# Split query and key products in the scores of a hybrid block, and half of a gate chunk computed earlier

## The reference, cut to what matters

```python
def mla_branch(c_q, c_kv, k_rope, cos, sin, ...):
    q = (rms_norm(c_q, q_norm) @ w_uq).reshape(B, S, 8, 64 + 32)
    q_nope, q_rope = q[..., :64], apply_rope(q[..., 64:], cos, sin)
    kv = (rms_norm(c_kv, kv_norm) @ w_ukv).reshape(B, S, 8, 64 + 64)
    k_nope, v = kv[..., :64], kv[..., 64:]
    k_rope = apply_rope(k_rope, cos, sin)
    s = (einsum('bhqd,bhkd->bhqk', q_nope, k_nope)
         + einsum('bhqr,bkr->bhqk', q_rope, k_rope)) * 96 ** -0.5
    p = softmax(where(key <= query, s, neg))
    return einsum('bhqk,bhkd->bhqd', p, v) ... @ w_o
merged = sigmoid(gate_a) * y_a + sigmoid(gate_b) * y_b
```

## Time and profile before

| | us |
|---|---|
| median of 3 runs | 1553.4 (1551.65 to 1553.79) |
| the profiled execution, its own time | 1557.54 |
| its span in the trace | 1555.8 |
| TensorE busy | 1513.7, 97% |
| VectorE busy | 1080.2, 69% |
| ScalarE busy | 659.0, 42% |
| GpSimd busy | 96.8, 6% |

### The profile page before, as it was taken

The page is one execution under the profiler, slowest core; times in us unless marked ns, Lnnn a source line. Parts: engine busy times, 40 slices in busy tenths (PEclk is TensorE's granted clock), DMA queues, the critical chain, the costliest instruction groups (busy, mean ns, idle before and its releaser), DMA issues.

```text
span 1555.8 us, 26174 instructions
## 1 busy us (share of the span) xinstructions
PE 1513.7 (97%) x10293; PEld 1219.9 (78%) x10293; DVE 1080.2 (69%) x1776; ACT 659.0 (42%) x1165; POOL 96.8 (6%) x181
## 2 busy tenths in 40 slices
PE   6999999999999999999999999999999999999998
PEld 5976666777777888788787887888888888888776
DVE  6468976467786581477866469777777757777786
ACT  7544454344433212445423236444444533333453
POOL 1010000000010001255100020000000000000000
PEclk9999999999999998999999999999999999999999
DMA  5020000713222535302346214444444688888754
GB/s 194 25 67 28 1 1 7 198 41 106 65 68 65 166 122 124 109 4 68 108 162 256 83 48 135 150 149 152 157 154 145 218 307 316 292 289 282 265 186 149
DMA packets 176752, 212.41 MB, mean 137 GB/s; under 512 B 28645, under 2 KB 110946, under 8 KB 176002
## 3 DMA queue, kind: packets, MB, share of 16 engines
q1 hardware_dynamic: 176574, 210.91, 40.9%
q10 hardware_dynamic: 68, 0.02, 0.0%
HBM read 154.11 MB, written 54.82 MB: 134 GB/s over the span
## 4 chain that ended last, share of the span: by engine, by line
PE 72%; DVE 13%; DMA 9%; issue 2%; ACT 2%; SPq 1%; DVEq 0%; ACTq 0%
PE bank L3255 19%; PE bank L2855 17%; DMA down_raw<-in_w_ff_down 6%; PE bank L3319 5%; PE bank L3167 5%; PE bank L3220 5%; PE bank L2755 3%; PE bank L2715 2%; PE bank L2648 2%; PE bank L2768 2%; PE bank L2783 2%; PE bank L2793 2%; DMA z_raw<-in_w_ff_down 2%; DVE yl L2482 1%; DVE mg_lo L2480 1%
## 5 line engine op out<-in xcount | busy, mean ns | idle before, releaser
L2855 PE MATMUL bank<-uT_hi,w_hi 128*128 128x512 f32 x432 | 172.3, 399 | 0.0
L2855 PE MATMUL bank<-uT_hi,w_lo 128*128 128x512 f32 x432 | 169.0, 391 | 0.0
L2855 PE MATMUL bank<-uT_lo,w_hi 128*128 128x512 f32 x432 | 168.9, 391 | 0.0
L3319 PE MATMUL bank<-mg_lo,mg_hi 128*128 128x512 f32 x576 | 135.7, 391 | 2.4 <-DVE mg_lo L2482 2.1
L3319 PEld LDWEIGHTS bank<-mg_lo,mg_hi 128*128 128x128 f32 x576 | 107.5, 188 | 27.8 <-DVE mg_lo L2482 5.6
L3319 PE MATMUL bank<-yh,mg_lo 128*128 128x512 f32 x384 | 119.1, 391 | 0.2
L1259 ACT ACTIVATE zbuf<-bank 128x512 f32<-128x512 f32 x54 | 32.3, 599 | 183.8 <-PE bank L2855 179.7
L2855 PEld LDWEIGHTS bank<-uT_hi,w_hi 128*128 128x128 f32 x432 | 81.6, 189 | 22.1 <-issue 5.2
L1606 ACT ACTIVATE f<-f 128x512 f32<-128x512 f32 x64 | 40.5, 632 | 131.6 <-DVE f L2434 69.6
L2855 PEld LDWEIGHTS bank<-uT_hi,w_lo 128*128 128x128 f32 x432 | 81.7, 189 | 17.4 <-issue 1.0
L2855 PEld LDWEIGHTS bank<-uT_lo,w_hi 128*128 128x128 f32 x432 | 81.6, 189 | 17.4
(11 more groups left out here) (497 smaller groups left out, 3778.4 us busy)
## 6 DMA issues: line engine op xcount, KB each, us to landing
down_raw<-in_w_ff_down SPq DMA_DIRECT2D x80, 512.0 KB, 5.5
down_raw<-f_spill SPq DMA_DIRECT2D x56, 512.0 KB, 4.2
f_spill<-x SPq DMA_DIRECT2D x80, 256.0 KB, 2.6
w_raw<-in_w_in SPq DMA_DIRECT2D x28, 512.0 KB, 4.2
sgate<-gate_spill SPq DMA_DIRECT2D x16, 512.0 KB, 4.4
up_a<-in_w_ff_up SPq DMA_DIRECT2D x16, 512.0 KB, 4.8
up_b<-in_w_ff_up SPq DMA_DIRECT2D x16, 512.0 KB, 4.2
f_spill<-f SPq DMA_DIRECT2D x32, 256.0 KB, 2.3
```

Source lines behind the costliest of these rows:

```text
L2855: ins = nc.tensor.matmul(ps[2 * slot + g][:], st[:, slot, k, :], mv[:, k, g * HALF:(g + 1) * HALF], start=(k == 0 and m == 0), stop=(k == ...
L3319: ins = nc.tensor.matmul(ps[4 * (q % 2) + t][:], st, mv_, start=(start and w == 0 and m == 0), stop=(stop and w == 1 and m == 2))
```

## The change

**Scores.** Each score product becomes three fp32r products with 128 rows. The stationary operands are `qh` (both 64-row halves hold the high part of the query), `ql` (its low part twice) and `qr3` (the rope rows four times, two groups of 32 rows with the high part and two with the low part); the moving ones are `kn` (high part of the key in one half of the rows, low part in the other) and `kr3` (rope rows of the key likewise). The query chunks are copied in one piece with the softmax scale in it, so that DVE's scaling of the maximum (L1904) goes. They are stored to DRAM chunk by chunk (`store_q`), loaded per query tile (`load_q`, two DMAs, and `load_q_rope`, four), and split by GpSimd (`q_split`, four operations for each tile, the tile's chunk of 1024 numbers a partition). The 17 spreading DMAs go. A tile's load waits for the scores of the tile two before. ACT copies a key chunk in two pieces, DVE then subtracts in two.

**Gate chunk.** Half of chunk two (24 matmuls, tokens 0 to 511) moves from behind the last unit into units 22 to 29, three each; its rounding and subtraction move from units 24 and 26 to unit 21. ACT copies the result at unit 31.

**Inverse.** `tt` and `xg` are zeroed whole by GpSimd, SP's loads of `tt` wait for that, and the products take 64 rows instead of 32, the added ones zero.

```diff
-        [(kind, g, j) for j in range(2) for kind in ("x", "rot")] + [(kind, g, j) for kind in ("q", "k") for j in range(NH // 2)]]
+        [(kind, g, j) for j in range(2) for kind in ("x", "rot")] + [(kind, g, j) for j in range(NH // 2) for kind in ("q", "k")]]
-BANKS = (2, 6, 7, 4, 5, 3, 0, 1)
+BANKS = 3 * (2, 6, 7, 4, 5, 3, 0, 1) + (2, 6, 7, 0, 4, 1, 5, 3)
...
+FILL2 = range(22, 30)
...
+                def q_split(i):
+                    b, low = i % 2, slice(2 * ROPE, 4 * ROPE)
+                    pool.wait_ge(*s_qt[b](32 * (i // 2 + 1)))
+                    pch(pool, nc.gpsimd.tensor_scalar(qh[b][:], qn[b][:], 1.0, 0.0, ALU.mult, ALU.add))
+                    nc.gpsimd.tensor_tensor(ql[b][:], qn[b][:], qh[b][:].bitcast(F32), ALU.subtract).then_inc(s_ql.sem, 1)
+                    pool.wait_ge(*s_qrt(64 * (i + 1)))
+                    pch(pool, nc.gpsimd.tensor_scalar(qr3[b][:], qr_in[:], 1.0, 0.0, ALU.mult, ALU.add))
+                    pool.wait_ge(*s_ql(i + 1))
+                    nc.gpsimd.tensor_tensor(qr3[b][low], qr_in[low], qr3[b][low].bitcast(F32), ALU.subtract).then_inc(s_rl.sem, 1)
...
-                for m in range(2):
-                    nc.gpsimd.memset(tt[CH * m + BL:CH * m + CH, :, 0:BL], 0.0).then_inc(s_z0z, 1)
+                nc.gpsimd.memset(tt[:], 0.0).then_inc(s_z0z, 1)
+                nc.gpsimd.memset(xg[:], 0.0).then_inc(s_z0z, 1)
...
-                        ins = nc.tensor.matmul(ps[b0 + g][:, 0:w], qT[0:QH, h, i * P:(i + 1) * P],
-                                               kT[0:QH, h, 512 * g:512 * g + w], start=True, stop=True)
+                    if h == 0:
+                        pe.wait_ge(*s_ql(i + 1))
+                        pe.wait_ge(*s_rl(i + 1))
+                    terms = ((qh[b][:, at[0], at[1], :], kn[:, h, :]), (ql[b][:, at[0], at[1], :], kn[:, h, :]), (qr3[b][:, h, :], kr3[:]))
+                    for m, (st, mv) in enumerate(terms):
+                        for g in range(halves(u)):
...
+                    if u in FILL2:
+                        if u == FILL2.start:
+                            pe.wait_ge(s_wcl, KD + 3)
+                        j = 3 * (u - FILL2.start)
+                        fill(3, 0, j, j + 3)
...
-                fill(2, 0, 0, 6)
+                fill(3, 1, 0, 6)
                 values(n)
...
-                fill(2, 0, 6, 3 * KD)
-                fill(3, 1, 0, 3 * KD)
+                fill(3, 1, 6, 3 * KD)
...
-                            rows = slice(CH * m + BL, CH * m + CH)
+                            rows = slice(CH * m, CH * m + CH)
```

171 lines of the change are left out of this document (122 added, 49 removed).

## The result

| | before | after |
|---|---|---|
| median of 22 runs each, in turn on one chip, us | 1553.12 (1548.49 to 1557.63) | 1558.18 (1550.76 to 1559.98) |
| ratio, 95% interval | | 1.0027 (1.0019 to 1.0035) |
| the profiled execution, its own time / its span | 1557.54 / 1555.8 | 1557.32 / 1555.6 |
| first mask of attention / mask of unit 63 | 112.37 / 261.66 | 115.52 / 270.77 |
| first product of the windows | 279.43 | 285.48 |

The change makes the kernel slower by 0.27%. I forecast 1547.6, a gain of 0.4%, in a range that ends at 1552.5. The forecast was wrong, and the time lies outside the range.

A forecast was written before the change was run, and what follows sets the result against it. TensorE, busy 97% of the span, was taken as the bound, with DVE's chain counting in T2 to T4. The terms summed to -5.8 us, giving 1547.6 from the median of 1553.4; range of 8 in 10: 1539.5 to 1552.5.

The forecast's parts named there:

- T5 to T7, -7.0: Attention tiles T5 to T7: cheaper score products save 0.24 to 0.34 us a unit, all of it TensorE's; minus 7.0 us.
- T4, -1.2: Attention tile T4, bound by DVE: without L1904 the chain is 0.15 us shorter a unit; minus 1.2 us.
- The way of the queries: Stores, loads and GpSimd's splits of queries: 11.2 us a tile, covered by a tile of attention; costed at nothing.
- The first split under the last projections: Before attention: GpSimd's first query split lies under the 24 last projections; costed at nothing.
- Unit 21, +3.0: Weight rounding moved to unit 21: weights land late and ACT, DVE, TensorE wait; plus 3.0 us (1.2 to 4).
- T3, +0.8 and +0.4 for units 22 and 23: Gate matmuls inside units: units 22 and 23 plus 0.4 us; T3, with units 24 to 29 at 2.32 us, plus 0.8.
- Behind attention, -2.8: After the last unit: 24 matmuls fewer are 5.5 us, but TensorE waits for the weight load; 2.8 us saved.
- +0.9 for the clock: Ahead of the first window: the 2.7 us pause can lower TensorE's clock; half of 1.7 us taken, plus 0.9.
- T0 and T1, units 16 to 20: Early attention: T0 plus 0.5 us (0 to 1.1), T1 minus 0.5, units 16 to 21 minus 0.9 by DVE's shorter chain.
- The narrow rival: Score products of 128 columns run at the plain rate, 0.645 us for three instead of 0.35: plus 3.7, 1551.3; alone 20%.
- The inverse, +1.0: Before the inverse: GpSimd's larger zeroing delays SP's loads, so the first product waits; plus 1.0 us (0 to 2).
- the clock rival: Around the inverse: twice the rows keep TensorE's clock up, bringing back 7 us: 1540.6; chance 23% alone.

## Why the prediction was wrong, point by point

**T5 to T7, -7.0; T4, -1.2.** The prices of the products were right, and T7 shows it (-2.16 of -2.7). The step that failed is "Nothing is late next: DVE needs 21.5 of 28.8 us in T7". It was read in the one tile in which GpSimd does nothing, and taken for three. In T4 to T6 DVE's minimum was held by GpSimd. With the hold gone, T4 is -1.15 (forecast -1.2), and T5 to T7 are -5.8 (forecast -7.0): sizes right to 1.2 us, sign right.

**The way of the queries, "I cost it at nothing".** Half of it was right: each split is done long before its tile. But I asked only whether the new work would be late, not whom it would hold. The page of the Trainium skill that I cited names the condition, two SBUF inputs, and I applied it with a false statement: "In attention only the gate's subtraction has" two inputs. L1903, which stood in the program before, has two, and it stands on the chain of each unit from T4 on. I also read the contention as something that lengthens the split; the profile after shows the split at its price (2.37 us whether anything waits or not) and DVE paying; the split does get longer, to 3.19, only where DVE's operation stands first. An estimate from these rows would have been: 24 minima in T4 to T6, GpSimd busy some 7 of 23 us in each, so seven of them meet it, each held for up to 2.4 us and some 1.2 on average: 8 us. The measured hold was 7.5, of which 6.1 reached the start of T7.

**The first split under the last projections.** The cover was there, and the loads cost nothing on GpSimd; but they were put into the queue ahead of stores that a two-buffer copy waits for, with a landing of 6.2 us instead of 2.4. This was +3.15 where I had 0. I had counted the loads' time and not what they do to the transfers beside them. With the loads moved it is +0.7 in the first such trace, and 0 to +1.9 in the six.

**Unit 21, +3.0 in a range of 1.2 to 4.** The mechanism was right, in the place forecast; it took 4.43, since the store landed in 4.5 us instead of 2.65, the end at which I had put "the store held up by SP's new loads".

**T3, +0.8 and +0.4 for units 22 and 23.** Measured +3.05 from unit 21 to 32. The part that I had not counted is the clock, at 0.53 for 3.4 us behind the stop: about 1.6 us. The rest is the mis-sized term: even with no stop and the clock up, the 24 products cost 4.4 us there against the same kernel without them. My 2.32 us for a unit took TensorE to be full and nothing else in the way.

**Behind attention, -2.8, and +0.9 for the clock.** The pause before the windows was 2.40 us for 2.7 forecast, the gain 3.06. The clock did not fall behind it in the profile after, 1.00 from 285.4 on, and that was luck. Six kernels here have this pause, 2.25 to 2.40 us. In three of them the clock stayed up, in three it fell for some 3.4 us, and the way to the inverse was some 1.6 us longer. The product behind the pause in one of the three, at nearly twice its usual length:

```profile
272.53 0.76 PE L2958 MATMUL bank<-uT_hi,w_hi 128*128 128x512 f32 x1 [2.25 <-DVE w_lo L2041]
```

So half of 1.7 was a fair term.

**T0 and T1, units 16 to 20.** T0 +0.57 (forecast +0.5), T1 -0.61 (-0.5), units 16 to 20 -0.64 (-0.7). For T0 the agreement is in part luck: with the clock at 1.00 it is 9.53 us with the old products and 9.74 to 9.76 with the new, +0.2, and its clock moves it by over 1 us from one execution to the next. The narrow rival fell with the 0.11 us between starts.

**The inverse, +1.0.** The first product waited 0.71 us for its loads, inside 0 to 2, and came 0.92 later behind the first window. But this was the small half: the clock rival, at 23%, is what happened here. In the two profiles it gave 6.6 us, near my 7; by the medians the whole part gave 3.7 and 4.0. The profile of before, from which I took the 17 us at the lower level, was an execution in which it cost more than in the others.

**The sum.** Up to the first window the terms gave -7.5 us and the profiles +6.05. Of the 13.5 between them 6.8 stand in T4 to T6 (mostly the held minimum), 3.15 at the front, 3.0 in the gate chunk (unit 20 to 32 and behind the last unit) and 0.5 in T7. Behind it, up to `gupt`, the profiles gave back 5.7 where I had +1.9; by the medians the inverse's part gave 3.7. The clock rival was right in its mechanism and had 1540.6 as its time, further off than the forecast, since what was lost ahead of the windows was in neither. The held minimum and the front were on no list of rivals but the 5% for "a stall that I do not see". The chance of 0.09 for slower was too small for a change that puts a new engine and a new stream of transfers beside the chain of each unit. The gate chunk's condition, "over 6 us in T2 and T3", was met: +7.5 from unit 20 to 32.

**What stays open.** The medians make the gate chunk's move 6.2 us, the trace up to the first window 3.8; the lower clock behind the pause, in three of six, is some 0.8 on average, and the rest is inside the intervals. Why the clock falls behind a pause in one execution and not in the next is not shown. What makes the last stretch of the program vary by over 5 us between executions was not tried. Whether the front's 2.5 us reach the end is not settled by the medians.

## What to carry to other kernels

When a change gives work to an idle engine, the price is not only whether that engine is in time: list every operation of VectorE with two SBUF inputs that may run beside it, however small, since a 0.16 us operation can wait for nearly the whole of GpSimd's (2.17 of 2.37 us here). Folding two neighbouring numbers by a reduction with one input avoids it at the same length. A gain read from one trace should be looked at beside its granted clock: the same code differed by 1.6 us between executions in units 25 to 29, and by 1.2 in T0. New transfers should stand behind the stores that a double buffer waits for, and work moved under a loop is covered only if each unit of the loop has room for it in order of time, not on average.

## What the runs showed of the hardware that I had not expected

- DVE's minimum with two SBUF inputs, 0.158 us alone, waits until GpSimd's running operation is over: up to 2.17 us, seven times of 32. GpSimd's operations with one input do it too. A reduction with one input does not wait (at most 0.16 us, eight overlaps). GpSimd's subtraction waits for DVE's with two SBUF inputs in turn, 3.19 us in place of 2.37.
- The granted clock depends on the rows that small products use. Two stages of 128 float32 products with 32 columns: at 32 rows stretches at 0.50, at 64 rows none, with zeroes in the added rows. It was worth 3.7 and 4.0 us by the medians, with the cost of the zeroing in it.
- The same pause of TensorE lowers the granted clock in one execution and not in another. At unit 26 1.85 us is followed by some 3.4 us at 0.50, and 1.82 us, with the same code, by none. The pause of 2.25 to 2.40 us ahead of the windows is followed by the lower level in three kernels of six, the stop of some 4 us at unit 21 in all four that have it.
- Query stores of 256 KB land in 2.3 to 3.0 us, and one in 6.2 with the loads of two tiles ahead of it in the queue; a 512 KB store lands in 4.5 us instead of 2.6 with six loads just ahead.
